# A hybrid encoder layer on one core: the first two weight chunks of the first feed-forward advance together, by quarters

## What is computed

```python
x = x + 0.5 * swiglu_ffn(rms_norm(x, ffn1_norm), ffn1_w_in, ffn1_w_out)
h = rms_norm(x, mix_norm)
# h @ w_in_proj -> q, k, v, a recurrent branch and its gate; attention and recurrence
x = x + concat([y_attn, y_rnn]) @ w_out_proj
x = x + 0.5 * swiglu_ffn(rms_norm(x, ffn2_norm), ffn2_w_in, ffn2_w_out)

def rms_norm(x, g):
    return x * rsqrt(mean(x * x, axis=-1) + EPS) * g

def swiglu_ffn(h, w_in, w_out):
    g, u = split(h @ w_in, 2, axis=-1)
    return (silu(g) * u) @ w_out          # 2816 hidden columns
```

## Time and profile before

| | us |
|---|---|
| median of 3 runs (942.10 to 943.39) | 942.45 |
| span of the profiled execution, first to last instruction | 940.4 |
| the median above that span: start and end around it | 2.05 |
| PE busy | 925.7 (98% of the span) |
| DVE busy | 482.5 (51%) |
| ACT busy | 331.2 (35%) |

### The profile page before, as it was taken

The page is one execution under the profiler, slowest core; times in us unless marked ns, Lnnn a source line. Parts: engine busy times, 40 slices in busy tenths (PEclk is TensorE's granted clock), DMA queues, the critical chain, the costliest instruction groups (busy, mean ns, idle before and its releaser), DMA issues.

```text
span 940.4 us, 11101 instructions
## 1 busy us (share of the span) xinstructions
PE 925.7 (98%) x4154; PEld 754.3 (80%) x4154; DVE 482.5 (51%) x712; ACT 331.2 (35%) x526; POOL 3.1 (0%) x25
## 2 busy tenths in 40 slices
PE   8999999999999999999998999999999999999998
PEld 6888888888888888777875678888888888888886
DVE  6754444454444345665879776645444444422321
ACT  7422222332223233356647654333222233212210
POOL 0000000000000000000000000000000000000000
PEclk9999999999999999999999999999999999999999
DMA  7222322222222234222221022222232222232240
GB/s 264 103 90 93 115 106 89 89 89 77 90 93 92 92 95 154 97 82 90 91 90 45 1 90 78 102 89 89 92 108 113 89 89 76 70 115 92 92 144 37
DMA packets 16295, 89.13 MB, mean 95 GB/s; under 512 B 2064, under 2 KB 2192, under 8 KB 8976
## 3 DMA queue, kind: packets, MB, share of 16 engines
q1 hardware_dynamic: 16128, 88.32, 26.9%
q0 software_dynamic: 144, 0.52, 0.2%
HBM read 86.74 MB, written 2.10 MB: 94 GB/s over the span
## 4 chain that ended last, share of the span: by engine, by line
PE 95%; DVE 2%; ACT 1%; DMA 1%; issue 1%; SPq 0%; ACTq 0%
PE bank L976 31%; PE bank L978 30%; PE bank L977 30%; PE bank L1173 1%; PE bank L1116 1%; PE bank L1150 1%; DMA x<-xT_dram 1%; PE bank L1163 0%; DVE h_lo L600 0%; PE bank L1090 0%; DVE small L897 0%; ACT w_hi L342 0%; PE bank L991 0%; ACT sq L519 0%; DVE yr_lo L804 0%
## 5 line engine op out<-in xcount | busy, mean ns | idle before, releaser
L976 PE MATMUL bank<-h_hi,w_hi 128*128 128x512 f32 x768 | 301.5, 393 | 1.4 <-DVE w_lo L588 1.0
L978 PE MATMUL bank<-h_hi,w_lo 128*128 128x512 f32 x768 | 298.9, 389 | 0.0
L977 PE MATMUL bank<-h_lo,w_hi 128*128 128x512 f32 x768 | 298.9, 389 | 0.0
L588 DVE TENSOR_TENSOR w_lo<-raw,w_hi 128x1024 fp32r<-128x1024 f32 (+1 forms) x178 | 188.7, 1101 | 81.3 <-ACT w_hi L342 75.7
L342 ACT ACTIVATE w_hi<-raw 128x1024 fp32r<-128x1024 f32 (+1 forms) x178 | 160.9, 951 | 162.4 <-PE bank L978 162.4
L976 PEld LDWEIGHTS bank<-h_hi,w_hi 128*128 128x128 f32 x768 | 144.2, 188 | 33.5 <-DVE w_lo L588 1.5
L977 PEld LDWEIGHTS bank<-h_lo,w_hi 128*128 128x128 f32 x768 | 144.2, 188 | 31.0 <-issue 1.2
L978 PEld LDWEIGHTS bank<-h_hi,w_lo 128*128 128x128 f32 x768 | 144.2, 188 | 30.2
L976 PE MATMUL bank<-act_hi,w_hi 128*128 128x512 f32 x352 | 138.7, 394 | 0.0
L978 PE MATMUL bank<-act_hi,w_lo 128*128 128x512 f32 x352 | 138.0, 392 | 0.0
L977 PE MATMUL bank<-act_lo,w_hi 128*128 128x512 f32 x352 | 136.6, 388 | 0.0
(11 more groups left out here) (173 smaller groups left out, 657.4 us busy)
## 6 DMA issues: line engine op xcount, KB each, us to landing
raw<-w_in_dram SPq DMA_DIRECT2D x43, 1024.0 KB, 4.8
raw<-w_out_dram SPq DMA_DIRECT2D x32, 704.0 KB, 4.0
raw<-w_qkv_dram SPq DMA_DIRECT2D x6, 1024.0 KB, 4.8
raw<-w_rnn_dram SPq DMA_DIRECT2D x4, 1024.0 KB, 4.8
raw<-w_proj_dram SPq DMA_DIRECT2D x4, 1024.0 KB, 4.7
x<-xT_dram SPq DMA_DIRECT2D x8, 256.0 KB, 6.4
out_dram<-x SPq DMA_DIRECT2D x8, 256.0 KB, 5.1
raw<-w_in_dram SPq DMA_DIRECT2D x4, 256.0 KB, 6.4
```

Source lines behind the costliest of these rows:

```text
L588: dve.tensor_tensor(w_lo[:, part], raw[:, part], w_hi[:, part].bitcast(F32), ALU.subtract).then_inc(low_made, 1)
L976: pe.matmul(dst, s_hi, m_hi, start=first, stop=False)
L977: pe.matmul(dst, s_hi, m_lo, start=False, stop=False)
L978: return pe.matmul(dst, s_lo, m_hi, start=False, stop=last)
```

## The change

Chunk 1 comes in four quarters too, and SP issues x0, quarter 0 of chunk 0, x1, quarter 0 of chunk 1, x2, quarter 1 of chunk 0, and so on to x7 and quarter 3 of chunk 1. ACT and DVE take one tile and one quarter in turn; from tile 3 on each also takes one square or one sum of squares a step, five of the eight being done within the steps and three behind them. The high and low parts of chunk 2 follow all of the squares. PE goes through both chunks by quarters: (0,0), (1,0), (0,1), (1,1), (0,2), (0,3), (1,2), the product with ones, and (1,3), where (c,q) is quarter q of chunk c, 12 matmuls each. The banks are those of before. The load of chunk 2 waits until the low parts of quarter (0,3) are made.

```diff
--- before.py
+++ after.py
@@ -194,7 +194,8 @@
         params_landed = [sem("cols_landed"), sem("params_landed")]
         bd_landed = sem("bd_landed")
 
-        quarter_landed = [sem(f"quarter_landed{q}") for q in range(3)]
+
+        quarter_landed = [[sem(f"quarter_landed{c}_{q}") for q in range(3)] for c in range(2)]
         quarter_high, quarter_low = sem("quarter_high"), sem("quarter_low")
         raw_landed = [sem("raw_landed0"), sem("raw_landed1")]
         high_made = sem("high_made")
...
@@ -263,21 +263,25 @@
             def load_x(i):
                 sp.dma_start(tile(x, i), xT[i]).then_inc(x_landed[i], 16)
 
-            def load(w, n, c, slot, size, first=False):
-
-                if not first:
-                    sp.wait_ge(low_made, c * 2 - 2)
+            def load(w, n, c, slot, size):
+
+                sp.wait_ge(low_made, c * 2 - 2)
                 sp.dma_start(raw[:, slot * SLOT:slot * SLOT + size], w[bass.ds(n * P, P), :]).then_inc(raw_landed[slot], 16)
 
+
+            def load_quarter(c, q):
+                part = slice(q * IN_COLS // 4, (q + 1) * IN_COLS // 4)
+                sp.dma_start(raw[:, c * SLOT + part.start:c * SLOT + part.stop],
+                             w_in1[c * P:(c + 1) * P, part]).then_inc(quarter_landed[c][q] if q < 3 else raw_landed[c], 16)
 
             for q in range(4):
                 load_x(2 * q)
-                part = slice(q * IN_COLS // 4, (q + 1) * IN_COLS // 4)
-                sp.dma_start(raw[:, part], w_in1[0:P, part]).then_inc(quarter_landed[q] if q < 3 else raw_landed[0], 16)
+                load_quarter(0, q)
                 load_x(2 * q + 1)
-            load(w_in1, 1, 1, 1, IN_COLS, first=True)
+                load_quarter(1, q)
             sp.dma_start(small[:, 0:TT].bitcast(I32), pos).then_inc(params_landed[1], 16)
             sp.dma_start(rows[:, :], rows_in).then_inc(params_landed[1], 16)
+            sp.wait_ge(low_made, 3)
             with sp.Fori(1, FFN_IN // 2) as i:
                 for s in range(2):
                     load(w_in1, i * 2 + s, i * 2 + (C_IN1 + s), s, IN_COLS)
@@ -377,18 +381,8 @@
 
             def ffn(f, size_next):
                 c0 = (C_IN1, C_IN2)[f]
-                def squares(first, last):
-                    for k in range(first, last):
-                        if k >= 2:
-                            act.wait_ge(sq_added, k - 1)
-                        square(k, k % 2)
-
-                if f == 0:
-                    squares(0, EARLY_SQUARES)
-                highs(c0 + 1, 1, IN_COLS)
-                if f == 0:
-                    squares(EARLY_SQUARES, KT)
-                    act.wait_ge(consts_made, CONSTS_FIRST)
+                if f == 1:
+                    highs(c0 + 1, 1, IN_COLS)
                 highs(c0 + 2, 0, IN_COLS)
                 root((1, 3)[f])
                 ffn_in_step(f, 0, 0, 0)
@@ -416,14 +410,27 @@
             act.wait_ge(consts_made, 1)
             bring_table(ACT.Copy)
             act.wait_ge(params_landed[0], 16)
+            def high_quarter(c, q):
+
+                act.wait_ge(quarter_landed[c][q] if q < 3 else raw_landed[c], 16)
+                part = slice(c * SLOT + q * IN_COLS // 4, c * SLOT + (q + 1) * IN_COLS // 4)
+                act.activation(w_hi[:, part], raw[:, part], ACT.Copy).then_inc((quarter_high, high_made)[q % 2], 1)
+
+            def first_square(k):
+
+                if k >= 2:
+                    act.wait_ge(sq_added, k - 1)
+                square(k, k % 2)
+
             for k in range(KT):
                 act.wait_ge(x_landed[k], 16)
                 gained(k, COL_G1)
-                if k % 2 == 0:
-                    q = k // 2
-                    act.wait_ge(quarter_landed[q] if q < 3 else raw_landed[0], 16)
-                    part = slice(q * IN_COLS // 4, (q + 1) * IN_COLS // 4)
-                    act.activation(w_hi[:, part], raw[:, part], ACT.Copy).then_inc((quarter_high, high_made)[q % 2], 1)
+                high_quarter(k % 2, k // 2)
+                if k >= 3:
+                    first_square(k - 3)
+            for k in range(KT - 3, KT):
+                first_square(k)
+            act.wait_ge(consts_made, CONSTS_FIRST)
             ffn(0, MIX_COLS)
 
 
@@ -716,11 +723,8 @@
                 dve.tensor_scalar(decay[:, RT:2 * RT], acc, -RG_C, None, ALU.mult).then_inc(decay_made, 1)
 
             def ffn(f, size_next):
-                for k in range(EARLY_SQUARES if f == 0 else 0):
-                    add_square(k, k % 2)
-                lows((C_IN1, C_IN2)[f] + 1, 1, IN_COLS)
-                for k in range(EARLY_SQUARES, KT if f == 0 else 0):
-                    add_square(k, k % 2)
+                if f == 1:
+                    lows(C_IN2 + 1, 1, IN_COLS)
                 lows((C_IN1, C_IN2)[f] + 2, 0, IN_COLS)
                 reciprocal_root((1, 3)[f])
                 ffn_in_step(f, 0, 0, 0)
@@ -738,14 +742,20 @@
 
             dve.wait_ge(params_landed[0], 16)
             dve.wait_ge(consts_made, CONSTS_FIRST)
+            def low_quarter(c, q):
+
+                dve.wait_ge((quarter_high, high_made)[q % 2], q // 2 * 2 + c + 1)
+                part = slice(c * SLOT + q * IN_COLS // 4, c * SLOT + (q + 1) * IN_COLS // 4)
+                dve.tensor_tensor(w_lo[:, part], raw[:, part], w_hi[:, part].bitcast(F32),
+                                  ALU.subtract).then_inc((quarter_low, low_made)[q % 2], 1)
+
             for k in range(KT):
                 gained(k, k, COL_G1)
-                if k % 2 == 0:
-                    q = k // 2
-                    dve.wait_ge((quarter_high, high_made)[q % 2], q // 2 + 1)
-                    part = slice(q * IN_COLS // 4, (q + 1) * IN_COLS // 4)
-                    dve.tensor_tensor(w_lo[:, part], raw[:, part], w_hi[:, part].bitcast(F32),
-                                      ALU.subtract).then_inc((quarter_low, low_made)[q % 2], 1)
+                low_quarter(k % 2, k // 2)
+                if k >= 3:
+                    add_square(k - 3, (k - 3) % 2)
+            for k in range(KT - 3, KT):
+                add_square(k, k % 2)
             ffn(0, MIX_COLS)
 
 
@@ -1000,37 +1010,52 @@
             def ffn(f):
                 c0 = (C_IN1, C_IN2)[f]
 
+                def first_pair():
+
+                    def quarter(c, q):
+                        pe.wait_ge((quarter_low, low_made)[q % 2], q // 2 * 2 + c + 1)
+                        for k in (2 * q, 2 * q + 1):
+                            pe.wait_ge(h_low, k + 1)
+                            for g in range(2):
+                                mm = product(bank[2 * c + g][:, :], weights(c, (2 * k + g) * P), parts(h_hi, h_lo, k * SEQ),
+                                             k == 0, k == KT - 1)
+                                if k == KT - 1:
+                                    mm.then_inc((g_done, chunk_used)[g], 1)
+
+                    pe.wait_ge(u_scaled, 2)
+                    for q in range(2):
+                        quarter(0, q)
+                        quarter(1, q)
+                    quarter(0, 2)
+                    quarter(0, 3)
+                    quarter(1, 2)
+                    sum_squares(1)
+                    quarter(1, 3)
+
                 def first_step():
 
                     for k in range(KT):
-                        if f == 0 and k % 2 == 0:
-                            pe.wait_ge((quarter_low, low_made)[k // 2 % 2], k // 4 + 1)
-                        if f == 1 and k % (KT // 2) == 0:
-                            pe.wait_ge(low_made, 2 * c0 + 1 + k // (KT // 2))
+                        if k % (KT // 2) == 0:
+                            pe.wait_ge(low_made, 2 * C_IN2 + 1 + k // (KT // 2))
                         if k == 0:
-                            pe.wait_ge(u_scaled, FT * f + 1)
-                        pe.wait_ge(h_low, 2 * KT * f + k + 1)
+                            pe.wait_ge(u_scaled, FT + 1)
+                        pe.wait_ge(h_low, 2 * KT + k + 1)
                         for g in range(2):
                             mm = product(bank[g][:, :], weights(0, (2 * k + g) * P), parts(h_hi, h_lo, k * SEQ),
                                          k == 0, k == KT - 1)
                             if k == KT - 1:
                                 mm.then_inc((g_done, chunk_used)[g], 1)
 
-                def in_step(i, s, meanwhile=None):
+                def in_step(i, s):
                     pe.wait_ge(low_made, i * 4 + 2 * ((C_IN1, C_IN2)[f] + s + 1))
                     pe.wait_ge(u_scaled, i * 2 + (FT * f + s + 1))
-                    if meanwhile:
-                        in_tile(s, 0, bank[2 * s][:, :], g_done, range(KT - 2))
-                        meanwhile()
-                        in_tile(s, 0, bank[2 * s][:, :], g_done, range(KT - 2, KT))
-                    else:
-                        in_tile(s, 0, bank[2 * s][:, :], g_done)
+                    in_tile(s, 0, bank[2 * s][:, :], g_done)
```

(5 more changed lines are left out.)

## The result

The changed kernel takes 946.48 us (median of 5 runs, 945.71 to 946.75) against 943.03 us before (5 runs, 942.10 to 943.39). The ratio is 1.0038, 95% interval 1.0027 to 1.0050: 3.45 us slower. The forecast was 944.0 with a range up to 946.0, so the time lies 0.5 us above the range. Two executions more of the kernel before stand in this comparison than in the table ahead of the prediction, and they put its median at 943.03 instead of 942.45. In the profiled execution the span is 944.7 us, against 940.4.

What follows compares the result with a forecast made beforehand. PE was taken to bound the kernel, meeting the emptied bank at 32.1 us. Gaps of -1.7 us and a new wait for L622 of +3.3 gave +1.6 on 942.45, so 944.0 us, range 943.2 to 946.0.

Steps and rivals of the forecast that it cites:

- What bounds the kernel: Whole span: PE, busy 98%; at 32.1 us PE's end of the pair and DVE's emptying of bank 1 arrive together.
- The gaps of the feed go, -1.7 us: Chunks 0 and 1: PE's waits for a quarter (0.49 us) and chunk 1's low parts (1.19 us) disappear.
- The product with ones behind 84 matmuls, the root at 27.7, chunk 2 at 33.75, +1.6 us: End of the pair: product ends 2.3 us later; -1.7 gaps and +3.3 new wait for L622 give +1.6 us.
- the 2.13: DVE from tile 3 on: one h_lo, one w_lo and one sum take 2.13 us a step.
- The landings: Feed: the n-th piece lands when the n-th landed before, 0.68 us a piece; (0,1) at 9.85, last at 16.4.
- the 0.8 us of cover: PE in the pair: smallest distance between data made and data needed, at quarter (0,1), 0.8 us.
- The step that failed: PE's 3.3 us standstill before chunk 2: extra price taken as nothing, the nearest row being a 1.4 us wait.
- the first rival: Behind the new wait: the clock falls to about half rate, losing 1.5 to 3 us; 945.5 to 947, chance 0.15.
- its upper half: Upper part of the falling-clock rival's 945.5 to 947 us, left out of the range 943.2 to 946.0.
- The row of full clock in the earlier trace: Kernel before, profile page: granted clock at full speed in all 40 slices.
- the 2.05 us of the prediction: Base of the forecast: profiled span 2.05 us shorter than the median of the runs, untouched by the change.
- the half rate of the earlier trace: Kernel's start: PE, having stood still until 2.7 us, ran at about half its rate for some 3 us.

Runs made afterwards that it cites:

- The two runs with banks 6 and 7: Chunk 2 in free banks 6 and 7, chunk 3's high and low parts earlier: changed kernel 940.47 us (0.9979); kernel before 942.02 us (0.9996).
- the late product: Kernel before with only the product with ones moved behind 84 of the pair's 96 matmuls instead of 66: 947.25 us, ratio 1.0051.
- the early product: Changed kernel with the product with ones ahead of quarter (1,2), behind 72 matmuls: 945.70 us, ratio 1.0035.
- the small products in the wait: Changed kernel with 14 small products of ones by ones behind the pair, into a bank nobody reads: 944.03 us, ratio 1.0018.
- the kernel with the banks and the small products in the attention: Changed kernel with chunk 2 in banks 6 and 7, plus 2, 5 and 4 small products in PE's first three attention waits: 940.33 us, ratio 0.9976.
- the last experiment: The changed kernel run again as it is, on the chip of its group: 945.97 us, ratio 1.0038.
- the short filling: Changed kernel with 5 small products behind the pair instead of 14: 945.78 us, ratio 1.0038.

## Why the prediction was wrong

**What bounds the kernel**, and that two things arrive together at 32.1: right. The two runs with banks 6 and 7 show it from both sides.

**The gaps of the feed go, -1.7 us**: right. The pair has no gap, and the two runs with the banks differ by 1.55 us in the median, about that.

**The product with ones behind 84 matmuls, the root at 27.7, chunk 2 at 33.75, +1.6 us**: right in every time. By itself the late product does it in the old kernel, 1.0051. That the table and the high parts of chunk 2 lie 0.3 us before it was in the working too, and the early product showed it. With two ends so near each other it is partly luck that the root came out at 27.7: in the first profile ACT was the later of the two, in the last the product. On DVE a step took 1.87 us instead of the 2.13 that had been added up from durations, so the sums were ready at 23.6 instead of 24.3; nothing waited for them.

**The landings**: quarter (0,1) was waited for until 10.29 against 9.85 in my list. It stayed within the 0.8 us of cover, and from (1,1) on ACT waited for no piece of the pair. The 0.68 us a piece of the prediction hold from the fifth piece to the eleventh (4.1 us for six); from the third to the fifth the same rows give 1.07, and (0,1), the sixth, was read off as if the faster pace held there.

**The step that failed** is the one on a PE that stands still for 3.3 us: "I take nothing, since the nearest row is the 1.4 us". It cost 1.43 us in the profile, and with the small products in the wait the clock stayed full there and the ratio went from 1.0038 to 1.0018. The mechanism stood there as the first rival, at 945.5 to 947 with a chance of 0.15, and its upper half was left out of the range; it is what happened, in both profiles of the changed kernel. Two readings led there. The row of full clock in the earlier trace rows came from an execution that is not the usual one: of the 43 executions of the kernel before that are compared in the two groups of experiments only 6 had a mean clock of 1.000, the others 0.996 to 0.998, so the clock falls in that kernel too. No profile shows where; in the kernel before with the banks 6 and 7 it falls in the attention, from 499 us. The base of the forecast comes from the same execution: in all executions on record the time is 1.7 to 1.9 us above the span, so the profiled one of before took 942.1 to 942.3 us, below both medians (942.45 and 943.03), and the 2.05 us of the prediction are not a fixed cost around the span. And the 1.4 us of the earlier trace rows were taken as a wait that the clock bears. It is the same wait in the attention (1.45 us) at which the clock fell in other profiles. The Trainium skill's rule (TensorE: Matmul & The Clock Gate, section Why this matters for your kernels) that long idle gaps between bursts bring half the clock is borne out by the traces (0.50 behind 3.48 us here); I had given it too little. Its limit for such a gap is longer than the 2.25 us that were enough here, and the measurement decides.

**A second, smaller term was missing.** The first product starts at 7.16 in the profile before, at 7.77 and 7.81 in two variants of the old order, and at 7.19 to 7.82 in seven profiles of the changed order. The landing of quarter 0 doesn't explain the late ones. The twelve products of ones ahead of it do. In the profile before:

```profile
2.67 4.62 PE L1055 MATMUL bank<-ones 128*128 128x128 f32 x24 [2.67 <-POOL ident L310]
6.41 0.69 DVE L747 TENSOR_TENSOR w_lo<-raw,w_hi 128x512 fp32r<-128x512 f32 x1 [0.74 <-ACT w_hi L426]
```

In the profile of the kernel with the banks and the small products in the attention:

```profile
2.67 5.49 PE L1096 MATMUL bank<-ones 128*128 128x128 f32 x24 [2.67 <-POOL ident L314]
6.08 0.69 DVE L760 TENSOR_TENSOR w_lo<-raw,w_hi 128x512 fp32r<-128x512 f32 x1 [0.34 <-ACT w_hi L422]
7.81 0.77 PE L997 MATMUL bank<-h_hi,w_hi 128*128 128x512 f32 x1
```

The low part of quarter 0 is made 0.33 us earlier in the second, and yet the first product starts 0.65 us later, since the 24 records of the ones take 5.49 us instead of 4.62. It is the half rate of the earlier trace rows, which lasts longer in some executions; the prediction had its rows on the table and asked only whether it comes back behind the wait. In the profile before that low part ends at 7.10 and lets the product start. In the seven profiles with a first product at 7.44 or later it ends by 7.23 in six; the seventh, of the last experiment, has a late landing as well (7.56).

The old order absorbs a late start in its gaps: with a first product at 7.81 the wait for the low parts of chunk 1 was 0.55 us instead of 1.04. The changed order has no gap before the product with ones and passes it on: with 7.82 chunk 2 starts at 34.45 instead of 33.78.

```profile
34.45 0.50 PE L986 MATMUL bank<-h_hi,w_hi 128*128 128x512 f32 x1 [3.32 <-DVE up_s L629]
```

So the sum should have read: 1.6 for the wait, 1.4 to 1.6 for the clock, and up to 0.7 for a late first product, 3.0 to 3.9 us, against 3.45 and 3.6 measured. The last term comes from a few profiles and was not made the subject of a run. What the second fall adds to the 3.45 stays open: four of the five executions of that comparison had a mean clock of 0.995, and the one with 0.998 was the fastest, at 945.71.

## What to carry to other kernels

Before a start-up is packed more densely, follow the chain that frees the resource the next step needs; work moved ahead of that chain's one instruction on PE delays it by its own length, and the gaps it closes come back behind it as one. Don't take a price of nothing from a wait shorter than the one you expect: here each wait of 2.25 us or more in the stream of products brought 1.4 to 1.6 us of half clock on top of its length. Read the clock in more than one execution, and in short stretches, before calling it full. Where the wait can't go, small products that fill it to its end keep the clock (14 of them did here, 5 won nothing); the better way is to take the wait away, as the free banks did.

## What the runs showed of the hardware

The granted clock fell to 0.50 behind 3.5, 3.3, 3.15 and 2.25 us of idle time, and in the attention behind a stretch whose longest single wait is 1.45 us. In the profile before and in two others the same waits in the attention passed without a fall. Each time it stayed low for 3.4 us, or for 6.8 in the attention of three profiles. It did not always fall at once: in the first profile of the changed kernel it fell 0.3 us before PE had started again, with the short filling 0.6 us after that, and with the early product (1.4) and in the changed kernel's other profile (1.5) over 1 us after, in the middle of dense work. Float32 products of 128x128 ones that filled the wait were enough to keep it up.
